# One ring for all PSUM banks and pairs in an eight-core decoder step, and a narrower wait ahead of its down projections

## The chip, the cores and the metric

The kernel runs on the 8 cores of one Trainium2 chip. Each core works on its own tokens with all weights, and no core talks to another. Five engines run side by side on a core: TensorE (PE, matmuls), VectorE (DVE), ScalarE (ACT), GpSimd (POOL, here only the issue of weight loads) and SyncE (SP, the issue of all other transfers). They wait for each other by semaphores only. TensorE writes its results to PSUM, which has 8 banks of 128 partitions x 512 fp32; VectorE or ScalarE must have read a bank before TensorE may write it again. The metric is the device time of one execution in microseconds, that of the slowest core; less is better.

## What is computed

One layer over 2048 prompt tokens and 128 sample tokens a core, width 1024. The reference, cut to what matters:

```python
def swiglu(x, w_gate, w_up, w_down):
    return (jax.nn.silu(x @ w_gate) * (x @ w_up)) @ w_down          # hidden width 2816

def layer(x, p_emb, conv_prev, ...):
    h = x + 0.5 * rmsnorm(swiglu(rmsnorm(x, ffn1_pre_g), ...), ffn1_post_g)
    n = rmsnorm(h, mix_pre_g)
    proj = n @ w_in                                                 # b_a, c_a, h_a, u, v, 512 each
    conv_out, new_conv = causal_dwconv(conv_prev, c_a * h_a, conv_w)
    y_a = b_a * conv_out
    v_n = rmsnorm(v.reshape(B, L, HEADS_B, HEAD_DIM_B), v_norm_g)
    mixed = chunk_spatial_mix(v_n, w_s, b_s)                        # 128 positions a chunk
    y_b = (u * mixed)
    y = jnp.concatenate([rmsnorm(y_a, out_g_a), rmsnorm(y_b, out_g_b)], axis=-1) @ w_out
    h = h + rmsnorm(y, mix_post_g)
    h = h + 0.5 * rmsnorm(swiglu(rmsnorm(h, ffn2_pre_g), ...), ffn2_post_g)
    gate = jax.nn.sigmoid(h @ ple_w_gate)
    h = h + rmsnorm(gate * (p_emb @ ple_w_proj), ple_post_g)
    return h, new_conv, v_cur
```

## The kernel before

The tokens of a core go through the whole layer in two passes: pass 0 has 9 blocks of 128 tokens in 3 tiles of 384, pass 1 has 8 blocks in 2 tiles of 512 (PASSES). A pass has these stages, and each engine does its part of them in the order in which the program is written:

- **Gate and up, feature-major** (gu_stage, gu_unit). Weights are the stationary operand, a tile of normalised tokens nT the moving one. A unit is a gate group and an up group of 8 matmuls, each into one bank from get_bank. ScalarE makes SiLU of the gate bank into one of two buffers sg, VectorE multiplies with the up bank into hmid (in tile "big"). The last product's event is kept in hm["ev"]. Weights lie in a ring of 8 slots; the first two or three are used for all tiles in turn, the others slot by slot.
- **Down, token-major** (tok_stage, proj_block). Per block, two banks make a pair (a tensor ps0 to ps3) from get_pair: 44 matmuls, then ScalarE squares the pair for the norm (post_stat), VectorE scales it into zsc and adds it to h (post_apply), and the next stage's norm makes a bf16 block nbr, which a transposing DMA on SP's queue brings into nT (pre_fn). The block waits for hm["ev"].
- **Mixer**: projections into single banks, a statistic by matmuls with ones (stat, line 707), the spatial mix (line 803), the product with u. The norm of a tile (norm_stat, norm_apply) is made one tile later; that of the last tile follows block 0 of the out projection (tail, with a bank from get_tp).
- **Out projection, token-major** (tok_stage with 16 matmuls a block), then the second gate and up and down stages as above.
- **Embedding stage** (ple), in groups of three blocks: three gate projections into pairs, a sigmoid of each on ScalarE; three embeddings (embed, 4 matmuls each) into pairs, the product on VectorE; then norm, add and y store. In pass 0 it also prepares pass 1: x_square squares the first input tile on ScalarE once its load has landed, x_stat sums it by 8 matmuls (line 498) into a bank from get_tp, which is held until x_apply has read it in the second group. The second tile of pass 1 is prepared inside the first gate and up stage of pass 1.

The hidden units of a stage lie in the same memory as the blocks that ple stores: guard1 makes the first products of pass 1 wait for the y stores of blocks 6, 7 and 8.

What decides who waits for a bank: there are three counters over the same 8 banks. get_bank takes all 8 in turn by rot["all"]; get_pair takes pairs ps0, ps1, ps2 by rot["pair"], always these three but in the last group of pass 1; get_tp takes the two banks of ps3 by rot["tp"]. Each goes on from where it last stood, whatever the others used meanwhile.

Of the kernel before, what the change touches and what calls it, by code (L numbers as in the profile page):

```python
# [14 lines left out]
NFF = 22  # L15
# [86 lines left out]
class Pass:  # L102
# [15 lines left out]
def build_program():  # L118
# [65 lines left out]
    rot = {"all": 0, "pair": 0, "tp": 0}  # L184

    def get_bank():
        b = banks[rot["all"] % 8]
        rot["all"] += 1
        assert b.free is not None
        PE.wait(b.free)  # L190
        b.free = None
        return b

    def get_tp():
        b = banks[6 + rot["tp"] % 2]
        rot["tp"] += 1
        assert b.free is not None
        PE.wait(b.free)
        b.free = None
        return b  # L200
# [222 lines left out]
    hm = {"ev": None}  # L423

    def gu_unit(P, f, fev, j0, ti, guard, hook=None):
# [3 lines left out]
        for jj in range(2):  # L429
# [60 lines left out]
    def x_stat(P, ti, sq, bank_of):  # L490
        c0, w = P.tiles[ti]
        bank = bank_of()
# [7 lines left out]
        e1 = act([ev], out=bank.t[:, 0:w], in_=bank.t[:, 0:w], func=AF.Ln, bias=EPS, scale=0.5)  # L500
        return bank, act([e1], out=bank.t[:, 0:w], in_=bank.t[:, 0:w], func=AF.Exp, scale=-0.5)
# [29 lines left out]
    def proj_block(P, b, nk, lhs, per, fl, wait, release_as_used, npair=3):  # L531
        pair = get_pair(npair)
# [50 lines left out]
    def mixer(P):  # L583
# [119 lines left out]
        def stat(sqs, w, bank_of=get_bank):  # L703
            bank = bank_of()
# [127 lines left out]
        def tail(ev):  # L832
            norm_apply(nt - 1, norm_stat(nt - 1, get_tp))
# [7 lines left out]
    def ple(P, N, base, pT_ev, groups):  # L841
# [8 lines left out]
        def embed(b, last, npair=3):  # L850
            pair = get_pair(npair)
# [12 lines left out]
        for gi, grp in enumerate(groups):  # L864
# [4 lines left out]
            if early:  # L869
                emb = {b: embed(b, b == grp[-1], 4) for b in grp}  # L870
            for b in grp:
                pair, ev = proj_block(P, b, 8, lambda k, b=b: nT_t[:, k, b * 128:(b + 1) * 128], 4, fg, [nT_ev[b]],
                                      lastg and b == grp[-1], 4 if early else 3)
# [5 lines left out]
                if N is not None and b == 1:  # L879
                    xs["sq"] = x_square(N, 0)  # L880
# [7 lines left out]
            if N is not None and gi == 1:  # L888
                x_apply(N, 0, *xs["st"], [gate_ev[3]])
# [3 lines left out]
            if N is not None and gi == 0:  # L893
                xs["st"] = x_stat(N, 0, xs["sq"], get_tp)
# [33 lines left out]
    def start_mid():  # L928
        x_apply(PASSES[0], 2, *x_stat(PASSES[0], 2, nx["sq"], get_bank))
# [14 lines left out]
    def next_mid():  # L944
        e = x_apply(PASSES[1], 1, *x_stat(PASSES[1], 1, nx["sq"], get_bank))
# [4 lines left out]
    for P in PASSES:  # L950
# [32 lines left out]
        tok_stage(P, NFF, 6, lambda b, k: hmid[:, k, b * 128:(b + 1) * 128], lambda b: [hm["ev"]],  # L983
# [31 lines left out]
        tok_stage(P, NFF, 6, lambda b, k: hmid[:, k, b * 128:(b + 1) * 128], lambda b: [hm["ev"]],  # L1015
                  base + G2POST, 4.0, 1, 0, cast, {8: next_x} if N is not None else None)
        gain_load(base + NGAIN + GMPRE, [h_ev[P.nb - 1]])
# [107 lines left out]
```

How the kernel before makes its waits and increments, by code:

```python
    def wait(self, *evs):  # L62
        best = {}
        for ev in _flat(evs, []):
            if ev.key not in best or best[ev.key].val < ev.val:
                best[ev.key] = ev
        for ev in best.values():
            if self.seen.get(ev.key, 0) >= ev.val:
                continue
            self.e.wait_ge(ev.sem, ev.val)
            self.seen[ev.key] = ev.val
            if _COLLECT is not None and ev.idx is not None:
                _COLLECT.add((ev.key, ev.idx))
# [1 line left out]
    def mark(self, ins):  # L75
        self.idx += 1
        if _USED is not None and (self.name, self.idx) not in _USED:
            return Ev(self.sem, self.n, self.name, self.idx)
        self.n += 1
        ins.then_inc(self.sem, 1)
        return Ev(self.sem, self.n, self.name, self.idx)
# [8 lines left out]
    def add(self, ins):  # L90
        self.n += 16
        ins.then_inc(self.sem, 16)
        return Ev(self.sem, self.n, self.name)
```

## Time and profile before

| | us |
|---|---|
| median of 3 runs (lowest, highest) | 1360.84 (1359.67, 1381.91) |
| the profiled execution | 1360.08 |
| its span on the slowest core, core 2 | 1359.0 |
| spans of the eight cores | 1348.5 to 1359.0 |
| TensorE busy | 1300.9 |
| VectorE busy | 523.6 |
| ScalarE busy | 410.3 |
| mean DMA rate | 103 GB/s |

Times in the rows below are microseconds from the start of core 2's span. A row of instructions in order of time has its start, its length, engine, line, operation and operands, how many were merged, and in brackets the idle time of the engine ahead of it and what ended that. A matmul's end is modelled. In pass 0 the first down projection runs from 205 to 291, the out projection from 381 to 416, the second from 591 to 676, the embedding stage to 723; in pass 1 they start at 891, 1043, 1234 and 1310.

### The profile page before, as it was taken

How to read it: one execution, taken by the hardware profiler on the slowest of the kernel's cores; microseconds unless marked ns; L12 is line 12 of the kernel's file. 1: busy time of each engine (PE TensorE's matmuls, PEld its weight loads, DVE VectorE, ACT ScalarE, POOL GpSimd, SP SyncE). 2: the span in 40 equal slices, each digit the busy share in tenths (PEclk: the TensorE clock that was granted, in tenths of full speed). 3: DMA queues.
4: the chain of work that ended last, by engine and by line, in shares of the span. 5: the costliest groups of instructions: out<-in, count | busy, mean ns of one | idle time of the engine just before them, and what ended most of it. 6: DMA issues, size and time to landing. Idle time of an engine off the chain costs nothing.

```text
span 1359.0 us, 18605 instructions; the slowest of 8 cores (1348.5 to 1359.0 us)
## 1 busy us (share of the span) xinstructions
PE 1300.9 (96%) x6770; PEld 650.7 (48%) x6770; DVE 523.6 (39%) x691; ACT 410.3 (30%) x858; POOL 94.3 (7%) x185
## 2 busy tenths in 40 slices
PE   6999999999989999999998999999999799999995
PEld 5566654455535666644433344444444344444442
DVE  3322223357776222213356322124467822212337
ACT  3311112344455111111165211123434611111136
POOL 1100000001001100000001000000010010000000
PEclk8999999999989999999989899999999899999998
DMA  9998322129715963231299983421396297433223
GB/s 214 180 211 181 63 47 47 28 57 164 129 26 103 169 108 63 48 69 26 53 201 232 224 160 67 75 43 31 68 166 116 57 158 143 78 56 62 32 39 124
DMA packets 88185, 139.87 MB, mean 103 GB/s; under 512 B 58272, under 2 KB 58528, under 8 KB 87456
## 3 DMA queue, kind: packets, MB, share of 16 engines
q0 software_dynamic: 25296, 90.25, 40.2%
q1 hardware_dynamic: 62800, 48.43, 13.6%
q8 instruction: 56, 0.92, 0.3%
q14 instruction: 33, 0.27, 0.1%
HBM read 206.03 MB, written 9.51 MB: 159 GB/s over the span
## 4 chain that ended last, share of the span: by engine, by line
PE 84%; DVE 6%; DMA 4%; issue 3%; ACT 2%; DVEq 0%; SPq 0%; ACTq 0%
PE ps L218 55%; PE ps L553 24%; PE ps L542 3%; DVE nT L227 2%; DVE zsc L227 2%; DMA h<-xT 1%; DVE big L231 1%; DMA y<-big 1%; DVE big L227 1%; DMA big<-xT 1%; ACT sg L223 1%; PE ps L498 1%; DVE nbr L227 1%; ACT big L223 1%; ACT L223 0%
## 5 line engine op out<-in xcount | busy, mean ns | idle before, releaser
L218 PE MATMUL ps<-nT,ring 128*128 128x384 bf16 (+1 forms) x4160 | 779.5, 349 | 18.8 <-DVE zsc L227 9.1
L218 PEld LDWEIGHTS ps<-nT,ring 128*128 128x128 bf16 x4160 | 407.9, 98 | 386.3 <-issue 35.4
L231 DVE TENSOR_TENSOR big<-ps,sg 128x384 bf16<-128x384 f32 (+1 forms) x220 | 134.1, 611 | 495.2 <-PE ps L218 476.0
L553 PE MATMUL ps<-ring,big 128*128 128x512 bf16 x1320 | 285.5, 379 | 4.4 <-DVE big L231 4.4
L223 ACT ACTIVATE sg<-ps 128x384 f32<-128x384 f32 (+1 forms) x237 | 126.8, 536 | 508.9 <-PE ps L218 499.9
L553 PEld LDWEIGHTS ps<-ring,big 128*128 128x128 bf16 x1320 | 128.9, 98 | 160.8 <-issue 6.0
L259 POOL DMA_DIRECT2D ring<-w x170 | 89.9, 537 | 1088.4 <-PE ps L218 499.6
L223 ACT ACTIVATE big<-ps 128x1024 bf16<-128x1024 f32 (+4 forms) x88 | 75.3, 870 | 222.6 <-PE ps L553 189.9
L227 DVE SCALAR_TENSOR_TENSOR zsc<-ps,st,gains 128x1024 f32<-128x1024 f32 x51 | 65.4, 1282 | 192.0 <-ACT st L223 191.7
L553 PE MATMUL ps<-ring,nT 128*128 128x512 bf16 x480 | 108.3, 386 | 5.7 <-DVE big L231 5.7
L553 PEld LDWEIGHTS ps<-ring,nT 128*128 128x128 bf16 x480 | 47.4, 99 | 65.6 <-issue 12.0
L231 DVE TENSOR_TENSOR big<-ps,big 128x384 f32<-128x384 f32 (+3 forms) x77 | 50.1, 686 | 46.3 <-PE ps L858 22.7
L231 DVE TENSOR_TENSOR h<-h,zsc 128x1024 f32<-128x1024 f32 x51 | 62.5, 1226 | 5.7 <-DVE zsc L227 0.5
L227 DVE SCALAR_TENSOR_TENSOR nbr<-h,st,gains 128x1024 bf16<-128x1024 f32 x34 | 43.6, 1282 | 36.9 <-ACT st L223 36.9
L223 ACT ACTIVATE nbr<-h 128x1024 bf16<-128x1024 f32 x34 | 35.9, 1057 | 60.3 <-DVE h L231 52.0
L223 ACT ACTIVATE st<-st 128x1 f32<-128x1 f32 x204 | 41.4, 203 | 18.2 <-ACT st L223 0.4
L542 PE MATMUL ps<-ring,big 128*128 128x512 bf16 x176 | 38.6, 379 | 0.0
L223 ACT ACTIVATE big<-big 128x384 bf16<-128x384 f32 (+2 forms) x44 | 25.0, 604 | 39.6 <-DVE big L231 37.1
L223 ACT ACT_TABLE_LOAD x25 | 32.1, 1283 | 13.5 <-PE ps L553 5.9
L218 PE MATMUL ps<-ring,nT 128*128 128x512 bf16 x136 | 30.2, 379 | 0.0
L227 DVE SCALAR_TENSOR_TENSOR nT<-big,gc,zsc 128x384 bf16<-128x384 f32 (+1 forms) x40 | 23.9, 666 | 9.0 <-ACT zsc L223 9.0
L542 PEld LDWEIGHTS ps<-ring,big 128*128 128x128 bf16 x176 | 17.2, 98 | 20.8
(65 smaller groups left out, 365.2 us busy)
## 6 DMA issues: line engine op xcount, KB each, us to landing
ring<-w POOLq DMA_DIRECT2D x170, 512.0 KB, 14.3
h<-x SPq DMA_DIRECT2D x17, 512.0 KB, 28.0
y<-big SPq DMA_DIRECT2D x13, 512.0 KB, 3.4
gains<-gain SPq DMA_DIRECT2D x12, 512.0 KB, 10.0
h<-xT SPq DMA_DIRECT2D x3, 1536.0 KB, 16.6
big<-xT SPq DMA_DIRECT2D x2, 2048.0 KB, 14.7
y<-zsc SPq DMA_DIRECT2D x4, 512.0 KB, 2.9
big<-pT POOLq DMA_DIRECT2D x2, 512.0 KB, 8.0
```

The costliest lines, as they stand in the source:

```text
L218: ins = nc.tensor.matmul(out_ap, l, r, start=(i == 0), stop=(i == n - 1))
L223: return ACT.mark(nc.scalar.activation(**kw))
L227: return DVE.mark(nc.vector.scalar_tensor_tensor(out=out, in0=in0, scalar=scalar, in1=in1, op0=op0, op1=op1))
L231: return DVE.mark(nc.vector.tensor_tensor(out=out, in0=in0, in1=in1, op=op))
L259: nc.gpsimd.dma_start(out=ring_t[:, s, o:o + HALF], in_=w_d[f % NFILL, :, o:o + HALF])))
L498: ins = nc.tensor.matmul(bank.t[:, 0:w], ones_t[:], sqt[:, k, :], start=(k == 0), stop=(k == 7))
L542: ins = nc.tensor.matmul(o.t, lhs(k), sv[:, k % per, half * 512:half * 512 + 512], start=(k == 0), stop=(k == nk - 1))
L553: ins = nc.tensor.matmul(o.t, lhs(k), sv, start=(k == 0), stop=(k == nk - 1))
```

## The change

All PSUM banks and pairs now come from one counter, rot["n"]. get_bank takes the next bank, get_pair the next pair of an even and an odd bank, leaving one out where the counter is odd; so a pair stage goes over all four pairs, and what is handed out is always what was handed out longest ago, but for a bank left out. get_tp is gone. In the embedding stage of pass 0 the statistic of pass 1's first tile no longer holds a bank: x_stat writes its Ln and Exp to the first half of a gain slot (dst), and the gain that belongs there is loaded after x_apply instead of at the end of the down stage. x_square there stands behind the third sigmoid instead of the second, and waits for the last block's h (guards["zsc"]). Last, gu_unit keeps the product's event per tile, and a down block waits for that of its own tile.

```diff
     def __init__(self, idx, rows, tiles, sample):
...
+    def tile_of(self, b):
+        return [ti for ti in range(len(self.tiles)) if b in self.blocks(ti)][0]
...
-    rot = {"all": 0, "pair": 0, "tp": 0}
-
-    def get_bank():
-        b = banks[rot["all"] % 8]
-        rot["all"] += 1
+    rot = {"n": 0}
+
+    def take(b):
         assert b.free is not None
         PE.wait(b.free)
         b.free = None
         return b
 
-    def get_tp():
-        b = banks[6 + rot["tp"] % 2]
-        rot["tp"] += 1
...
-    def get_pair(n=3):
-        i = rot["pair"] % n
-        rot["pair"] += 1
-        lo, hi = banks[2 * i], banks[2 * i + 1]
-        assert lo.free is not None and hi.free is not None
-        PE.wait(lo.free, hi.free)
-        lo.free = hi.free = None
-        return ps[i], lo, hi
+    def get_bank():
+        i = rot["n"] % 8
+        rot["n"] += 1
+        return take(banks[i])
+
+    def get_pair():
+        i = (rot["n"] + 1) // 2 % 4
+        rot["n"] = 2 * i + 2
+        return ps[i], take(banks[2 * i]), take(banks[2 * i + 1])
...
-            hm["ev"] = tt([ev_s, evl, guard(j)], hmid[:, j, cols], bu.t[:, 0:w], sg_t[:, si, 0:w], ALU.mult)
-            bu.free = hm["ev"]
-            sg_free[si] = hm["ev"]
+            e = hm[ti] = tt([ev_s, evl, guard(j)], hmid[:, j, cols], bu.t[:, 0:w], sg_t[:, si, 0:w], ALU.mult)
+            bu.free = sg_free[si] = e
...
-        e1 = act([ev], out=bank.t[:, 0:w], in_=bank.t[:, 0:w], func=AF.Ln, bias=EPS, scale=0.5)
-        return bank, act([e1], out=bank.t[:, 0:w], in_=bank.t[:, 0:w], func=AF.Exp, scale=-0.5)
+        if dst is None:
+            e1 = act([ev], out=bank.t[:, 0:w], in_=bank.t[:, 0:w], func=AF.Ln, bias=EPS, scale=0.5)
+            return bank, act([e1], out=bank.t[:, 0:w], in_=bank.t[:, 0:w], func=AF.Exp, scale=-0.5)
+        bank.free = e1 = act([ev], out=dst, in_=bank.t[:, 0:w], func=AF.Ln, bias=EPS, scale=0.5)
+        return Bank(dst), act([e1], out=dst, in_=dst, func=AF.Exp, scale=-0.5)
...
-                if N is not None and b == 1:
-                    xs["sq"] = x_square(N, 0)
+                if N is not None and b == 2:
+                    xs["sq"] = x_square(N, 0, [guards["zsc"]])
...
             if N is not None and gi == 1:
-                x_apply(N, 0, *xs["st"], [gate_ev[3]])
+                gain_load(base + NGAIN + GMPRE, [x_apply(N, 0, *xs["st"], [gate_ev[3]])])
...
             if N is not None and gi == 0:
-                xs["st"] = x_stat(N, 0, xs["sq"], get_tp)
+                xs["st"] = x_stat(N, 0, xs["sq"], gain(base + NGAIN + GMPRE)[:, 0:512])
...
-        tok_stage(P, NFF, 6, lambda b, k: hmid[:, k, b * 128:(b + 1) * 128], lambda b: [hm["ev"]],
+        tok_stage(P, NFF, 6, lambda b, k: hmid[:, k, b * 128:(b + 1) * 128], lambda b, P=P: [hm[P.tile_of(b)]],
                   base + G2POST, 4.0, 1, 0, cast, {8: next_x} if N is not None else None)
-        gain_load(base + NGAIN + GMPRE, [h_ev[P.nb - 1]])
         guards["zsc"] = h_ev[P.nb - 1]
```

TensorE's order at the out projection of pass 0, before: the last two products with u (into ps3 and ps0), block 0, the last tile's statistic (line 707), and blocks 1 to 3. "Waits" names the semaphores that stand ahead of a matmul: sem_dve is VectorE's, sem_act ScalarE's, slots are weights, t0 and t1 transposes.

```order
L218 MATMUL ps3<-nT,ring 128x384 [waits sem_dve]
L218 MATMUL ps3<-nT,ring 128x384 x7
L218 MATMUL ps0<-nT,ring 128x384 [waits sem_dve]
L218 MATMUL ps0<-nT,ring 128x384 x7
L553 MATMUL ps0<-ring,nT 128x512 [waits sem_dve,slot6_0,slot6_1]
L553 MATMUL ps0<-ring,nT 128x512 x3
L553 MATMUL ps0<-ring,nT 128x512 [waits slot7_0,slot7_1]
L553 MATMUL ps0<-ring,nT 128x512 x11
L707 MATMUL ps3<-big,ones 128x384 [waits sem_act] x4
L553 MATMUL ps1<-ring,nT 128x512 x16
L553 MATMUL ps2<-ring,nT 128x512 x16
L553 MATMUL ps0<-ring,nT 128x512 [waits sem_dve]
```

The same place after the change:

```order
L212 MATMUL ps1<-nT,ring 128x384 [waits sem_dve]
L212 MATMUL ps1<-nT,ring 128x384 x7
L212 MATMUL ps1<-nT,ring 128x384 [waits sem_dve]
L212 MATMUL ps1<-nT,ring 128x384 x7
L549 MATMUL ps2<-ring,nT 128x512 [waits sem_dve,slot6_0,slot6_1]
L549 MATMUL ps2<-ring,nT 128x512 x3
L549 MATMUL ps2<-ring,nT 128x512 [waits slot7_0,slot7_1]
L549 MATMUL ps2<-ring,nT 128x512 x11
L703 MATMUL ps3<-big,ones 128x384 [waits sem_dve,sem_act]
L703 MATMUL ps3<-big,ones 128x384 [waits sem_act] x3
L549 MATMUL ps0<-ring,nT 128x512 [waits sem_dve]
L549 MATMUL ps0<-ring,nT 128x512 x15
```

Block 0 stands in ps2 instead of ps0, which the last product with u has just been using, the statistic in the low bank of ps3, and block 1 in ps0.

TensorE's order from the last block of pass 1's out projection (line 542) into its second gate and up stage, before:

```order
L542 MATMUL ps0<-ring,nT 128x512 [waits sem_dve]
L542 MATMUL ps0<-ring,nT 128x512 x15
L218 MATMUL ps0<-nT,ring 128x512 [waits sem_dve,slot4_0,t1,t0]
L218 MATMUL ps0<-nT,ring 128x512 x7
L218 MATMUL ps1<-nT,ring 128x512 x8
L218 MATMUL ps1<-nT,ring 128x512 [waits slot4_1]
L218 MATMUL ps1<-nT,ring 128x512 x7
L218 MATMUL ps2<-nT,ring 128x512 x8
L218 MATMUL ps2<-nT,ring 128x512 [waits slot5_0]
L218 MATMUL ps2<-nT,ring 128x512 x7
```

And after:

```order
L538 MATMUL ps1<-ring,nT 128x512 [waits sem_dve]
L538 MATMUL ps1<-ring,nT 128x512 x15
L212 MATMUL ps2<-nT,ring 128x512 [waits sem_dve,slot4_0,t1,t0]
L212 MATMUL ps2<-nT,ring 128x512 x15
L212 MATMUL ps3<-nT,ring 128x512 [waits sem_dve,slot4_1]
L212 MATMUL ps3<-nT,ring 128x512 x15
L212 MATMUL ps0<-nT,ring 128x512 [waits sem_dve,slot5_0]
L212 MATMUL ps0<-nT,ring 128x512 x15
L212 MATMUL ps1<-nT,ring 128x512 [waits sem_dve,slot5_1]
L212 MATMUL ps1<-nT,ring 128x512 x15
```

The first gate group was in ps0, the pair of the last block itself; now it is in ps2, and the last block's ps1 comes round as the fourth pair.

ScalarE's order in the first group of pass 0's embedding stage, before (big<-ps are sigmoids, big<-big the squares of x_square, sg,st<-big the norm's squares, ps<-ps the Ln and Exp of x_stat):

```order
L223 ACTIVATE big<-ps 128x1024 x2
L223 ACTIVATE big<-big 128x1024 x4
L223 ACTIVATE big<-ps 128x1024
L223 ACTIVATE sg,st<-big 128x1024
L223 ACTIVATE st<-st 128x1 x2
L223 ACTIVATE sg,st<-big 128x1024
L223 ACTIVATE st<-st 128x1 x2
L223 ACTIVATE sg,st<-big 128x1024
L223 ACTIVATE st<-st 128x1 x2
L223 ACTIVATE ps<-ps 128x512 x2
```

And after:

```order
L217 ACTIVATE big<-ps 128x1024 x3
L217 ACTIVATE big<-big 128x1024 x4
L217 ACTIVATE sg,st<-big 128x1024
L217 ACTIVATE st<-st 128x1 x2
L217 ACTIVATE sg,st<-big 128x1024
L217 ACTIVATE st<-st 128x1 x2
L217 ACTIVATE sg,st<-big 128x1024
L217 ACTIVATE st<-st 128x1 x2
L217 ACTIVATE gains<-ps 128x512
L217 ACTIVATE gains<-gains 128x512
```

The third sigmoid moved ahead of the four squares, and Ln and Exp write gains.

## Rows read from the trace of the kernel before

**Rows 1.** The page, its head and part 1.

```profile
span 1359.0 us, 18605 instructions; the slowest of 8 cores (1348.5 to 1359.0 us)
...
PE 1300.9 (96%) x6770; PEld 650.7 (48%) x6770; DVE 523.6 (39%) x691; ACT 410.3 (30%) x858; POOL 94.3 (7%) x185
```

**Rows 2.** TensorE's waits: total us, times, longest us.

```profile
PE ps L553 <- DVE big L231: 10.0, 6, 4.3
PE ps L218 <- DVE zsc L227: 9.1, 3, 7.0
```

**Rows 3.** TensorE in order of time, pass 0.

```profile
204.96 76.13 PE L553 MATMUL ps<-ring,big 128*128 128x512 bf16 x352 [1.02 <-DVE big L231]
...
381.02 6.48 PE L553 MATMUL ps<-ring,nT 128*128 128x512 bf16 x16 [4.29 <-DVE big L231]
...
387.98 24.34 PE L553 MATMUL ps<-ring,nT 128*128 128x512 bf16 x112
...
421.99 167.86 PE L218 MATMUL ps<-nT,ring 128*128 128x384 bf16 x1032 [0.96 <-DVE zsc L227]
```

**Rows 4.** TensorE in order of time, pass 1.

```profile
891.24 66.64 PE L553 MATMUL ps<-ring,big 128*128 128x512 bf16 x308 [1.16 <-DVE big L231]
...
1042.99 3.61 PE L553 MATMUL ps<-ring,nT 128*128 128x512 bf16 x16 [1.40 <-DVE big L231]
...
1047.30 20.88 PE L553 MATMUL ps<-ring,nT 128*128 128x512 bf16 x96
...
1078.59 154.35 PE L218 MATMUL ps<-nT,ring 128*128 128x512 bf16 x704 [6.95 <-DVE zsc L227]
```

**Rows 5.** TensorE in order of time, from pass 0 to pass 1.

```profile
691.97 1.87 PE L858 MATMUL ps<-ring,big 128*128 128x512 bf16 x4 [3.38 <-ACT big L223]
693.63 3.62 PE L498 MATMUL ps<-big,ones 128*128 128x512 bf16 x8
...
728.80 15.34 PE L218 MATMUL ps<-nT,ring 128*128 128x512 bf16 x64 [5.38 <-DVE big L231]
...
753.58 0.38 PE L218 MATMUL ps<-nT,ring 128*128 128x512 bf16 x1 [0.79 <-DVE nT L227]
```

**Rows 6.** Busy time by stretch: all engines, then TensorE's granted clock, DMA share, GB/s.

```profile
1080.00:1084.00 4.00, 4.00 (x13) 1.42 (x11) 1.93 (x2) 3.30 (x6) 0.13 (x1) 0.60 0.35 68
```

**Rows 7.** VectorE and ScalarE in order of time, 364 to 436, pass 0.

```profile
371.88 2.68 DVE L227 SCALAR_TENSOR_TENSOR big<-ps,gc,bbc 128x256 f32<-128x256 f32 x8
...
378.71 1.94 DVE L231 TENSOR_TENSOR big<-ps,big 128x384 f32<-128x384 f32 x4
...
380.78 1.33 ACT L223 ACTIVATE big<-big 128x384 bf16<-128x384 f32 x3
...
426.95 0.87 ACT L223 ACTIVATE sg<-ps 128x384 f32<-128x384 f32 x2
```

**Rows 8.** ScalarE, SP and VectorE in order of time, 664 to 762.

```profile
687.03 3.90 ACT L223 ACTIVATE big<-big 128x1024 bf16<-128x1024 f32 x4 [2.49 <-DMA big<-xT]
...
732.18 5.38 SPq L901 DMA_DIRECT2D y<-big  x3
...
752.08 0.69 DVE L231 TENSOR_TENSOR big<-ps,sg 128x512 bf16<-128x512 f32 x1 [2.57 <-DMA y<-big]
```

**Rows 9.** DMA issues, 737.1 to 737.6 (block 8's store): count, KB, us to landing.

```profile
y<-big SPq DMA_DIRECT2D x1, 512.0 KB, 14.8
```

**Rows 10.** DMA queues, 744 to 746: packets, MB, share; q0 weights, q1 SP.

```profile
q0 software_dynamic: 75, 0.25, 74.6%
q1 hardware_dynamic: 71, 0.28, 36.1%
```

**Rows 11.** ScalarE in order of time, 1030 to 1090.

```profile
1072.73 1.06 ACT L223 ACTIVATE nbr<-h 128x1024 bf16<-128x1024 f32 x1 [0.38 <-DMA nT<-nbr]
```

**Rows 12.** Transposes of that stretch: us from issue to landing.

```profile
DMA to landing us min/median/max: 3.0/3.0/9.8
```

**Rows 13.** Chain of work that ended last: start, us, what.

```profile
1346.69 1.23 DVE big L231
```

More of the change, by code:

```diff
@@ L192, in get_bank @@
         return b
-    def get_tp():
-        b = banks[6 + rot["tp"] % 2]
-        rot["tp"] += 1
[L197 to L200, printed above, removed]
-    def get_pair(n=3):
-        i = rot["pair"] % n
-        rot["pair"] += 1
-        lo, hi = banks[2 * i], banks[2 * i + 1]
-        assert lo.free is not None and hi.free is not None
-        PE.wait(lo.free, hi.free)
-        lo.free = hi.free = None
-        return ps[i], lo, hi
+    def get_bank():
[6 more added lines that the diff above has]
+        return ps[i], take(banks[2 * i]), take(banks[2 * i + 1])
     def mm_group(out_ap, pairs, wait=None, kwait=None):
@@ L422, in build_program @@
     sgc = {"i": 0}
-    hm = {"ev": None}
+    hm = {}
     def gu_unit(P, f, fev, j0, ti, guard, hook=None):
@@ L488, in x_square, with x_stat @@
         return sq
-    def x_stat(P, ti, sq, bank_of):
+    def x_stat(P, ti, sq, dst=None):
         c0, w = P.tiles[ti]
-        bank = bank_of()
+        bank = get_bank()
         sqt = x_sq_at(P, ti)
@@ L529, in post_apply, with proj_block @@
         return e
-    def proj_block(P, b, nk, lhs, per, fl, wait, release_as_used, npair=3):
-        pair = get_pair(npair)
+    def proj_block(P, b, nk, lhs, per, fl, wait, release_as_used):
+        pair = get_pair()
         pt, lo, hi = pair
@@ L701, in square, with stat @@
             return i, e
-        def stat(sqs, w, bank_of=get_bank):
-            bank = bank_of()
+        def stat(sqs, w):
+            bank = get_bank()
             for c, (i, e) in enumerate(sqs):
@@ L832, in tail @@
         def tail(ev):
-            norm_apply(nt - 1, norm_stat(nt - 1, get_tp))
+            norm_apply(nt - 1, norm_stat(nt - 1))
         return norm_ev, tail, vo_ev["ev"]
@@ L849, in ple, with embed @@
             pay_owed([nT_ev[P.nb - 1]], NFILL + 1)
-        def embed(b, last, npair=3):
-            pair = get_pair(npair)
+        def embed(b, last):
+            pair = get_pair()
             pt, lo, hi = pair
@@ L869, in ple @@
             if early:
-                emb = {b: embed(b, b == grp[-1], 4) for b in grp}
+                emb = {b: embed(b, b == grp[-1]) for b in grp}
             for b in grp:
                 pair, ev = proj_block(P, b, 8, lambda k, b=b: nT_t[:, k, b * 128:(b + 1) * 128], 4, fg, [nT_ev[b]],
-                                      lastg and b == grp[-1], 4 if early else 3)
+                                      lastg and b == grp[-1])
                 gate_ev[b] = ev
@@ L914, in gb_guard @@
         return [guards["zsc"] if b % 6 >= 4 else None, out_ev.get(b - 6) if b >= 6 else None]
-    first = x_stat(PASSES[0], 0, x_square(PASSES[0], 0), get_bank)
+    first = x_stat(PASSES[0], 0, x_square(PASSES[0], 0))
     x_apply(PASSES[0], 0, *first)
-    second = x_stat(PASSES[0], 1, x_square(PASSES[0], 1), get_bank)
+    second = x_stat(PASSES[0], 1, x_square(PASSES[0], 1))
     warm_up(40)
@@ L928, in start_mid @@
     def start_mid():
[L929 removed]
+        x_apply(PASSES[0], 2, *x_stat(PASSES[0], 2, nx["sq"]))
     def start_loads():
```

8 lines of the change are left out of this document (4 added, 4 removed).

## Prediction

> **What bounds the kernel now.** I read the page first, then TensorE's waits, then its instructions in order of time, and last the engines it waits for. The page says that TensorE is busy for 1300.9 of 1359.0 us [rows 1]. So nothing but TensorE's pauses, and matmuls that run slower than others of their shape, can be won without taking matmuls away; the change takes none away. Its longest waits name VectorE, once through tile big and once through zsc [rows 2]: TensorE waits until VectorE has read a bank, or until VectorE has written the last FFN product. In order of time these pauses stand in four kinds of place. (a) At each of the four starts of a down projection: 1.02 us in pass 0 and 1.16 in pass 1 [rows 3, 4], one row of each pass shown. (b) Around the out projection of pass 0: 4.29 us ahead of its first block, and among others 0.96 in the gate and up matmuls behind it [rows 3]. (c) From the embedding stage of pass 0 into pass 1: 3.38, 5.38 and 0.79 us [rows 5]. (d) Around the out projection of pass 1: 1.40 and 6.95 us [rows 4]. Behind the long pauses the clock is at 1.2 GHz for a while: the 16 matmuls of block 0 take 6.48 us in pass 0 and 3.61 in pass 1 [rows 3, 4], and 1080 to 1084 has a granted clock of 0.60 [rows 6]. The pauses of 1.0 to 1.4 us are followed by matmuls at full pace.
>
> **Part 1: the product wait, (a).** A down block now waits for the products of its own tile. Tile 0's last product is four units of work older than the stage's last in pass 0 and two in pass 1, so it is long done, and the pair is the oldest of the ring, used four units ago. The pauses go: 1.02 twice and 1.16 twice. A row's modelled end lies some 0.16 us past the next start (1042.99 + 3.61 is 1046.60, yet four matmuls of 20.88 / 96 us each stand between it and 1047.30 [rows 4]), so a pause costs 0.16 more than it shows. 4 x 0.16 + 4.36 = **5.0**. Nothing stands between these points and the end but TensorE, so all of it arrives.
>
> **Part 2: out projection of pass 0, (b).** Block 0 waited for pair ps0, one bank of which the last product with u still read. In the ring it takes ps2, last read by the mix operations that end at 371.88 + 2.68 = 374.56 [rows 7], while TensorE is free at 381.02 - 4.29 = 376.73. It starts there, at full clock, and ends at 380.0. But behind it stands the statistic of the last tile, whose four matmuls need ScalarE's squares, and these end at 380.78 + 1.33 = 382.11, because VectorE's products end only at 378.71 + 1.94 = 380.65 [rows 7]. So a new pause of 2 us stands there, and block 1 starts at 382.4 instead of 387.98: 5.6 earlier. VectorE's and ScalarE's work of the stage hangs on that statistic and moves by the same 5.6. The gate and up matmuls now start 128 matmuls of 24.17 / 112 us behind block 1's start, at 387.98 + 27.6 - 5.6 = 410.0, and find each pair free, but after 8 groups of 8 matmuls (167.86 us over 1032, so 1.30 a group) the ring is round at 420.4, and bank 0 is free only when ScalarE has made the first SiLU: 426.95 + 0.45 - 5.6 = 421.8 [rows 7]. The stage thus runs as if begun at 411.5. Before, the fourth group began at 421.99, as if begun at 418.1. Gain **6.6**.
>
> **Part 3: embedding stage into pass 1, (c).** The third embedding waited 3.38 us since its pair was freed by a sigmoid that stood behind the four squares of pass 1's input, and these wait for a load until 687.03 [rows 8]. The sigmoid now goes first, so the embedding starts at 688.6; the squares end one sigmoid later, 687.03 + 3.90 + 1.0 = 691.9, and the statistic's last matmul follows at 692.4. The next gates start at 692.6 instead of 693.63 + 3.62 = 697.2 [rows 5]; I take 4.3. Everything up to pass 1 moves with it, and the 5.38 us bank wait ahead of pass 1 goes too, so TensorE reaches pass 1 about 10 us earlier. This is not kept. The second tile of pass 1 waits for its normalised input, which VectorE writes only after the product of 752.08, and that one waits for the y store of block 8 (the unit's output lies where that store reads) [rows 8]. At 753.58 TensorE is already waiting for VectorE [rows 5]. The three stores were issued from 732.18 on, and the last landed 14.8 us after its issue [rows 8, 9]. So the second tile starts when the stores land, and these move with their issue, by 4.3. TensorE's other 6 us become a pause between its eighth bank and the first product. Gain **4.3**.
> The ring order puts a 0.5 MB gain load between the input load and the first of those stores. In 2 us of that time SP's queue moved 0.28 MB and the weight queue 0.25 [rows 10], so 0.5 MB may cost 3.6 us if nothing else gives. I take nothing, since three stores need only 10.8 us at that pace and have 14.8 behind the last issue alone, so the queue has gaps to give; 3.6 stays for the range.
> The Trainium skill (DMA: Bandwidth & Descriptors, Queues, rings and completion order) says that an engine takes turns between queue rows by packet and takes one ring's descriptors in order. The 71 and 75 packets agree [rows 10]. By that rule alone the moved load delays all six later stores, the gain of this part would be 0.7 instead of 4.3, and the whole 1339.3; that is rival A.
>
> **Part 4: out projection of pass 1, (d).** Block 0 no longer waits; the statistic needs squares that end some 0.4 us after block 0. Block 1 starts at 1045.9 instead of 1047.30: 1.4, and VectorE's chain moves as much. The gate and up matmuls waited 6.95 us for the pair of block 7. In the ring that pair is the last they need. What they need first is the transposed block 3, on which ScalarE's instruction at 1072.73 waited [rows 11], so it lands at 1072.6; 1.4 less is 1071.2. So the start goes from 1078.59 to 1071.3, and the pause ahead of it shrinks to 1.2, below those that left the clock alone. Before, about 4.6 us (1078.59 to 1083.2, by the granted clock [rows 6]) ran at half pace: 2.3 lost. Together 7.3 + 2.3 = 9.6. The second tile is wanted 12 groups of 1.73 us later, at 1092.0; block 7's transpose takes 9.8 us where the others take 3.0 [rows 12], since it runs beside the pT load, and lands at 1092.3. That takes back 0.4. Gain **9.2**.
>
> **What gains nothing.** In the last groups of pass 1 the ring removes a short wait, but VectorE is at the b5 block's add until 1346.69 and takes the next embedding with no pause of its own [rows 13]: the tail is VectorE's and ScalarE's, not TensorE's. The statistic's Ln and Exp write SBUF instead of a bank; no row of theirs is on TensorE's way.
>
> **Sum.** 5.0 + 6.6 + 4.3 + 9.2 = 25.1 off a span of 1359.0, so 1333.9. That execution took 1360.08, and the median of the runs is 1360.84, 0.8 more. 1360.84 - 25.1 = **1335.7**, 1.8% faster. A measurement of this kernel can tell about 2% from no change, which is 1333.6 or less.
>
> **The rivals.**
> A, the stores don't move (chance 0.17). For it: the moved gain load, and DMA engines that are full while weights come. Against it: the gaps. The second tile starts at 753 as now: 25.1 - 4.3 = 20.8 gained, 1340.0.
> B, the clock falls in the new pauses (0.15). The statistics of parts 2 and 3 now trickle over 2.4 and 3 us behind squares. Price of a fall: 6.48 - 3.61 = 2.9 us each [rows 3, 4]. For it: pauses of 3.38 and more did it. Against it: those up to 1.4 did not. Both: 25.1 - 5.8 = 19.3, 1341.5; one: 1338.6.
> C, the ring gives nothing (0.04): VectorE and ScalarE set the pace of the out projections, so TensorE only reaches full banks 8 groups later. Against it: in part 2 this costs 1.4 us, worked out above. Only part 1 stays: 1355.8. The Trainium skill (TensorE: Matmul & The Clock Gate, HAM oscillation) reports of one kernel that double buffering in PSUM gave no further gain. Here the trace disagrees, since 6.95 us are spent on one pair.
> D, the stores land earlier still (0.12): without gaps the three take 10.8 us from their first issue at 728, and with some us to get going the last is down by 744, not 747.7. Then the second tile gains 8.5, not 4.3: 29.3, 1331.5.
> E, slower than before (0.02): with fewer pauses the eight cores draw more at once and the clock granted to long stretches falls. At 1300.9 us busy it decides from 1.9% on (25.1 us), and at 4% it would cost 52 and give 1388. No long stretch shows it now.
> F, the forecast (0.50), with its own range of 1332.5 to 1339.
>
> **How the numbers follow.** F's upper part, A and B lie up to 1341.5; the range goes to 1344 for A with one fall of the clock (1342.9), and down to 1331 for D. It leaves out C, E and some of D and of the sums beyond. Below 1333.6 lie D and about a third of F: 0.28. Over 2% slower is E, 0.02. The rest, 0.70, is within 2%.
>
> **What would show it.** Right: the four down starts without a pause; block 0 of pass 0's out projection at 3.5 us and about 2 us of pause behind it; the gate and up stage behind it with one pause of 1 to 2 us at its ninth group; no pause at the third embedding; a pause of 4 to 6 us in pass 1's first tile that ends with a y store; pass 1's second FFN starting on the transpose. Wrong: matmuls of double length behind the statistics (B), the first product of pass 1 more than 12 us behind its store's issue (A), or a bank wait in the middle of a stage.

## The result, and the profile after

| | before | after |
|---|---|---|
| median of 4 runs, us | 1360.26 | 1335.69 |
| lowest run, us | 1357.31 | 1334.43 |
| ratio of the times, 95% interval | | 0.983 (0.9813 to 0.9847) |
| span on the slowest core | 1359.0 (core 2) | 1335.0 (core 7) |
| spans of the eight cores | 1348.5 to 1359.0 | 1329.7 to 1335.0 |

By the ratio the change makes the kernel 1.7% or 23.1 us faster (20.8 to 25.4 by its interval); the medians differ by 24.6, and 25.1 were forecast. The number hides one term that failed: most of what TensorE won on its way into pass 1 was lost again to three stores, and something else made up for it. Some runs of each kernel were disturbed on a die and have longer times; the ratio leaves them out, so it is what I compare below, one experiment in which every run was so has none, and where a profile has such a die only the other cores are read. The page and the waits of TensorE, as in [rows 1, 2]:

```profile
span 1335.0 us, 18647 instructions; the slowest of 8 cores (1329.7 to 1335.0 us)
...
PE 1293.0 (97%) x6770; PEld 649.3 (49%) x6770; DVE 523.4 (39%) x691; ACT 410.5 (31%) x858; POOL 94.3 (7%) x185
```

```profile
PE ps L212 <- DVE big L225: 6.0, 2, 5.8
PE ps L212 <- DVE nT L221: 4.9, 11, 2.1
...
PE ps L212 <- ACT sg L217: 1.5, 1, 1.5
...
PE ps L212 <- DMA nT<-nbr: 1.2, 1, 1.2
```

The two long entries of [rows 2] are gone: nothing of line 549 (553 before) waits for VectorE any more, and no matmul waits for zsc. The 5.8 us are one new pause in pass 1's first tile; only the waits for the first inputs, at the start of the program, are longer in total (8.5 us, 8.9 before).

TensorE in order of time in pass 0, core 7; these rows answer to [rows 3]:

```profile
202.59 76.14 PE L549 MATMUL ps<-ring,big 128*128 128x512 bf16 x352
...
374.19 3.62 PE L549 MATMUL ps<-ring,nT 128*128 128x512 bf16 x16
377.65 0.32 PE L703 MATMUL ps<-big,ones 128*128 128x384 bf16 x1
379.06 1.15 PE L703 MATMUL ps<-big,ones 128*128 128x384 bf16 x3 [1.08 <-ACT big L217]
380.04 24.34 PE L549 MATMUL ps<-ring,nT 128*128 128x512 bf16 x112
...
407.67 10.56 PE L212 MATMUL ps<-nT,ring 128*128 128x384 bf16 x64
419.73 161.36 PE L212 MATMUL ps<-nT,ring 128*128 128x384 bf16 x992 [1.50 <-ACT sg L217]
```

The down projection starts without a pause. Block 0 of the out projection takes 3.62 us instead of 6.48, and the one pause of the gate and up stage comes after 64 matmuls, that is at the ninth group, and waits for the first SiLU. Pass 1, which answers to [rows 4], has lost its bank waits too; its second FFN starts on a transpose:

```profile
877.77 66.64 PE L549 MATMUL ps<-ring,big 128*128 128x512 bf16 x308
...
1028.33 3.61 PE L549 MATMUL ps<-ring,nT 128*128 128x512 bf16 x16 [0.20 <-issue]
...
1032.64 20.88 PE L549 MATMUL ps<-ring,nT 128*128 128x512 bf16 x96
...
1058.15 152.11 PE L212 MATMUL ps<-nT,ring 128*128 128x512 bf16 x704 [1.17 <-DMA nT<-nbr]
```

Between the passes ([rows 5]) the embeddings no longer wait, but the first tile of pass 1 now has a pause of 5.77 us, and the second tile starts with one of 2.05:

```profile
692.75 2.75 PE L854 MATMUL ps<-ring,big 128*128 128x512 bf16 x12
...
708.29 13.98 PE L212 MATMUL ps<-nT,ring 128*128 128x512 bf16 x64
...
730.50 8.60 PE L212 MATMUL ps<-nT,ring 128*128 128x512 bf16 x32 [5.77 <-DVE big L225]
741.14 0.38 PE L212 MATMUL ps<-nT,ring 128*128 128x512 bf16 x1 [2.05 <-DVE nT L221]
```

The same stretch on SP and VectorE. The three stores are issued from 717.35 on, 2.5 us apart, and three products wait for one each; the last is let go at 739.65 by a store issued at about 722.4 ([rows 8] has the one row of before):

```profile
717.35 5.38 SPq L897 DMA_DIRECT2D y<-big  x3
...
729.55 0.69 DVE L225 TENSOR_TENSOR big<-ps,sg 128x512 bf16<-128x512 f32 x1 [7.23 <-DMA y<-big]
...
734.38 1.29 DVE L225 TENSOR_TENSOR big<-ps,sg 128x512 bf16<-128x512 f32 x2 [4.13 <-DMA y<-big]
...
739.65 0.69 DVE L225 TENSOR_TENSOR big<-ps,sg 128x512 bf16<-128x512 f32 x1 [3.99 <-DMA y<-big]
```

Its issue, 722.3 to 722.6, with count, KB and us to landing, as in [rows 9]:

```profile
y<-big SPq DMA_DIRECT2D x1, 512.0 KB, 17.2
```

And the queues while the first two are waiting, 717 to 723 (packets, MB, share of 16 engines), as in [rows 10]; the third is issued in the last of these us:

```profile
q0 software_dynamic: 187, 0.66, 107.5%
q1 hardware_dynamic: 4, 0.00, 0.1%
```

For almost 6 us the stores move nothing: the weight queue has the engines. It moves only 0.66 MB in that time; why its own packets take so long no run shows. What it carries was issued from 710.65 on:

```profile
710.65 3.18 POOL L253 DMA_DIRECT2D ring<-w  x6 [31.19 <-PE ps L212]
```

Then the held-back weight loads, six of 0.5 MB, were let go, since pass 1's second input tile had landed: its load was issued at 693.06 and took 16.9 us. (The row names a matmul as what ended the wait; on four other cores it names that load.) Granted clock (third column from the end) on core 7 in that stretch; the columns are those of [rows 6]:

```profile
720.00:724.00 4.00, 3.73 (x17) 1.35 (x15) 2.22 (x2) 3.99 (x5) 0.00 (x0) 1.00 0.90 81
...
728.00:732.00 4.00, 1.50 (x4) 0.58 (x5) 0.69 (x1) 0.60 (x1) 0.00 (x0) 0.50 0.99 211
732.00:736.00 4.00, 4.00 (x16) 1.54 (x15) 1.29 (x2) 0.82 (x2) 1.05 (x2) 0.83 1.07 212
...
744.00:748.00 4.00, 3.78 (x9) 1.15 (x9) 2.81 (x5) 0.60 (x1) 0.00 (x0) 0.50 0.97 151
748.00:752.00 4.00, 4.00 (x15) 1.51 (x13) 0.69 (x1) 0.00 (x0) 0.00 (x0) 0.69 1.02 199
```

Behind both pauses TensorE is at 1.2 instead of 2.4 GHz for some us.

### The profile page after: what moved, and what is told of

Same layout as the page of the kernel before. It is cut to its first block, busy times and chain, and to the rows that moved or that the text cites. A ratio compares the mean times of both kernels' runs of the same rounds, so it can differ in the third digit from the quotient of the medians.

```text
span 1335.0 us, 18647 instructions; the slowest of 8 cores (1329.7 to 1335.0 us)
## 1 busy us (share of the span) xinstructions
PE 1293.0 (97%) x6770; PEld 649.3 (49%) x6770; DVE 523.4 (39%) x691; ACT 410.5 (31%) x858; POOL 94.3 (7%) x185
## 4 chain that ended last, share of the span: by engine, by line
PE 87%; DVE 5%; DMA 3%; issue 2%; ACT 2%; DVEq 0%; SPq 0%; ACTq 0%
PE ps L212 56%; PE ps L549 25%; PE ps L538 3%; DMA h<-xT 1%; DVE zsc L221 1%; DMA y<-big 1%; DVE nT L221 1%; PE ps L854 1%; DVE big L221 1%; DVE big L225 1%; DVE nbr L221 1%; PE ps L703 1%; ACT L217 0%; DMA nT<-nbr 0%; ACT big L217 0%
## 5 line engine op out<-in xcount | busy, mean ns | idle before, releaser
L549 PE MATMUL ps<-ring,nT 128*128 128x512 bf16 x480 | 105.2, 379 | 0.2 <-issue 0.2
L212 PE MATMUL ps<-ring,nT 128*128 128x512 bf16 x136 | 30.2, 379 | 0.0
L538 PEld LDWEIGHTS ps<-ring,big 128*128 128x128 bf16 x176 | 17.2, 98 | 20.8
L221 DVE SCALAR_TENSOR_TENSOR big<-big,gc 128x384 f32<-128x384 f32 (+3 forms) x48 | 24.8, 589 | 0.0
## 6 DMA issues: line engine op xcount, KB each, us to landing
big<-xT SPq DMA_DIRECT2D x2, 2048.0 KB, 12.4
```

What stands on the lines that cost most here:

```text
L212: ins = nc.tensor.matmul(out_ap, l, r, start=(i == 0), stop=(i == n - 1))
L221: return DVE.mark(nc.vector.scalar_tensor_tensor(out=out, in0=in0, scalar=scalar, in1=in1, op0=op0, op1=op1))
L538: ins = nc.tensor.matmul(o.t, lhs(k), sv[:, k % per, half * 512:half * 512 + 512], start=(k == 0), stop=(k == nk - 1))
L549: ins = nc.tensor.matmul(o.t, lhs(k), sv, start=(k == 0), stop=(k == nk - 1))
```

## The experiments

All were timed beside the kernel before, whose median was 1357.9 for the first four and 1358.2 for the last four. A difference between two of them is that of their ratios, 0.001 being 1.36 us; each ratio is good to some 2 us, so what is smaller rests on the stretches below. To see where in the program a difference lies I also read, on each core, the time from the start of one down projection to that of the next, in the profiled execution. A is the stretch from pass 0's first to its second, with the mixer and out projection of pass 0; B runs from there to pass 1's first, over the embedding stage and the first FFN of pass 1; C is as A for pass 1. Mean of the cores in us, and for B lowest and highest:

| kernel | ratio (95% interval) | A | B | C |
|---|---|---|---|---|
| before | 1 | 386.1 | 295.9 (293.2 to 300.4) | 342.5 |
| changed | 0.983 (0.9813 to 0.9847) | 378.4 | 294.4 (291.8 to 296.8) | 332.4 |
| product wait alone | 0.9964 (0.995 to 0.9978) | 383.6 | 294.0 (289.6 to 296.6) | 341.7 |
| squares early | 0.9839 (0.9825 to 0.9854) | 378.4 | 293.1 (291.1 to 294.9) | 332.4 |
| gain load late | 0.9829 (0.9815 to 0.9844) | 378.4 | 293.5 (291.9 to 294.3) | 332.3 |
| weight loads late | 0.9745 (0.973 to 0.9759) | 378.4 | 281.9 (281.7 to 282.2) | 332.4 |
| three pairs | 0.9849 (0.9831 to 0.9868) | 378.9 | 294.2 (293.6 to 294.6) | 334.9 |
| weight and gain loads late | 0.9745 (0.9729 to 0.9761) | 378.4 | 281.9 (281.7 to 282.1) | 332.4 |
| before, weight loads late | 0.9971 (0.9959 to 0.9984) | 386.2 | 291.8 (289.8 to 294.1) | 342.9 |
| youngest pair first (six cores) | none | 378.4 | 294.1 (292.1 to 294.7) | 339.8 |

In the changed kernel A and C are the same on all cores within 0.2 us; B is not. It is the stretch in which transfers decide, and it is the same on all cores, within 0.5 us, only in the two kernels that have both the ring and the late weight loads.

**The product wait alone.** The kernel before, with

```diff
-            hm["ev"] = tt([ev_s, evl, guard(j)], hmid[:, j, cols], bu.t[:, 0:w], sg_t[:, si, 0:w], ALU.mult)
+            hm["ev"] = hm[ti] = tt([ev_s, evl, guard(j)], hmid[:, j, cols], bu.t[:, 0:w], sg_t[:, si, 0:w], ALU.mult)
...
-        tok_stage(P, NFF, 6, lambda b, k: hmid[:, k, b * 128:(b + 1) * 128], lambda b: [hm["ev"]],
+        tok_stage(P, NFF, 6, lambda b, k: hmid[:, k, b * 128:(b + 1) * 128], lambda b, P=P: [hm[P.tile_of(b)]],
```

> The kernel before with part 1 alone: a down block waits for the last product of its own tile; the three counters for the banks stay. Theory of the prediction: the four down starts lose their pause, 5.0 us in all, and nothing else moves, so the time goes from 1360.3 to 1355.3 (ratio 0.9963). Rival: the two starts of pass 0 (2.4 us) lie ahead of the way into pass 1, where TensorE waits for transfers, and are given back there; then only the two starts of pass 1 count, 2.6 us, 1357.7 (ratio 0.998). A second rival: the three pairs are still handed out by their own counter, and one of the starts now waits for a bank instead, 1.0 to 1.2 us less gain for each such start.

Measured: 0.9964, which is 4.9 us less, and no pause ahead of the down projections. That is what the first theory says; 2.6 would be a ratio of 0.998, just outside the interval. The stretches are less even than the sum. By the four pauses A should be 1.2 shorter, B and C 1.3 each; they are 2.5, 1.9 and 0.8 shorter. In A the other 1.3 us are mostly something else: in the kernel before, five cores reach the out projection 177.7 us behind the start of the down projection and three 176.1, here all eight after 176.0 to 176.2. Why is not shown. So the pauses are gone, but that exactly their price arrives is not proven by this run.

**Squares early.** The changed kernel with

```diff
-                if N is not None and b == 2:
+                if N is not None and b == 1:
```

> The changed kernel with the squares of pass 1's first input behind the second sigmoid again, as in the kernel before (part 3's reordering undone, the rest kept). The prediction put 3.4 of part 3's 4.3 us down to the third sigmoid standing ahead of the squares: then the third embedding waits some 3 us again and the time is 1338 to 1339. Rival: with four pairs in one ring the third embedding takes the pair of the second gate, which the second sigmoid has freed, so the order on ScalarE no longer matters, and the time stays at 1335.7 within 1 us.

Measured: 0.9839 against 0.983, 1.2 us and inside both intervals, and no core has a pause ahead of an embedding. The rival holds. The prediction named the right pause and the wrong cure: it is gone because the ring has four pairs, so that the third embedding writes the pair whose sigmoid is the second, not the third. The order on ScalarE is worth nothing that shows in the time. In the changed kernel the next gates start 5.6 us behind the embeddings on every core (682.40 - 676.76 on core 7). With the old order it is 4.4 to 6.3 and 5.4 on the mean: less where the input had landed early (4.9 on core 3, 681.25 - 676.35), more where the statistic waits for it.

**Gain load late.** The load that the change had moved is issued behind the y stores:

```diff
-                gain_load(base + NGAIN + GMPRE, [x_apply(N, 0, *xs["st"], [gate_ev[3]])])
+                xs["ap"] = x_apply(N, 0, *xs["st"], [gate_ev[3]])
...
         gain_load(base + GPLE + 3, [nxt["stt"]])
+        if N is not None:
+            gain_load(base + NGAIN + GMPRE, [xs["ap"]])
```

> The changed kernel with the moved 0.5 MB gain load issued behind the y stores of pass 0 instead of ahead of the second group's. If it delays the stores that pass 1 waits for (rival A of the prediction), taking it away gives up to 3.6 us back: 1332.1. Theory after reading the changed kernel's trace: SP's queue has run empty before the last three stores are issued (nothing of it moves between 717 and 723 on core 7), so the load delays at most the input load beside it; 1335.0, 0 to 1.5 us better.

Measured: 0.9829 against 0.983; B is 0.9 shorter on the mean of the cores, less than the cores differ. Whether it is 0 or 1 us stays open. The 3.6 us of the prediction's bound (a ratio of 0.9804) lie outside the interval.

**Weight loads late.** The changed kernel, with the six weight loads that are let go ahead of pass 1's FFN let go by another event:

```diff
-            pay_owed([xt_ev[1, 1]])
+            pay_owed([out_ev[8]])
```

pay_owed lets the held-back loads go, in GpSimd's queue, once its event has come: before, the landing of pass 1's second input tile, here that of block 8's y store.

> The changed kernel with the six weight loads of 0.5 MB that were held back until the second input tile of pass 1 had landed now held back until the y store of block 8 has landed. Theory: what keeps pass 1's first tile waiting (5.8 + 2.1 us of pauses on core 7 and 4 to 6 us at half clock behind them) are the last three stores, 12 to 17 us each, and they are slow because the weight queue takes 70 to 120% of the DMA engines' time in that stretch. Without it a store lands in 4 to 6 us, TensorE goes through the first tile without a pause of over 1 us, and gate and up of pass 1 take 155 to 159 us instead of 167 to 169.5: 1323 to 1328 (ratio to the kernel before 0.973 to 0.976). Rival 1: the stores are slow for another reason: no change, 1335.7. Rival 2: the fourth weight slot comes too late, and TensorE waits for weights at about 750 instead: 1333 to 1340.

Measured: 0.9745, 34.6 us less than before and 11.5 less than the changed kernel, as the theory says. B falls by 12.5 on the mean, and its spread between cores from 5.0 to 0.5 us. TensorE on the slowest core, core 1:

```profile
709.83 13.98 PE L212 MATMUL ps<-nT,ring 128*128 128x512 bf16 x64
723.64 1.69 PE L491 MATMUL ps<-nT,ones 128*128 128x512 bf16 x6
725.68 0.59 PE L491 MATMUL ps<-nT,ones 128*128 128x512 bf16 x2 [0.35 <-ACT nT L217]
726.11 8.58 PE L212 MATMUL ps<-nT,ring 128*128 128x512 bf16 x39
```

The 5.77 us pause is gone. First the row of the weight loads, which block 8's store now lets go; then the three stores, issued from 718.88 to 723.9, with count, KB and us to landing, and the clock behind them:

```profile
727.41 3.17 POOL L253 DMA_DIRECT2D ring<-w  x6 [45.43 <-DMA y<-big]
```

```profile
y<-big SPq DMA_DIRECT2D x3, 512.0 KB, 2.8
```

```profile
724.00:728.00 4.00, 3.58 (x17) 1.32 (x15) 2.54 (x4) 3.84 (x5) 0.59 (x2) 1.00 0.79 241
728.00:732.00 4.00, 4.00 (x20) 1.81 (x19) 2.57 (x4) 3.51 (x6) 2.58 (x5) 1.00 0.66 116
```

A store now lands 2.8 us after its issue (median of the three, the others 2.6 and 3.9), not 12 to 17, and the clock stays at 2.4 GHz. Both rivals are out: the stores were slow for the weight loads' sake, and the weights, issued at 727.4, come in time, since no matmul of core 1 waits for them.

**Three pairs.** The changed kernel with one counter, but projections over three pairs:

```diff
-    def get_pair():
-        i = (rot["n"] + 1) // 2 % 4
+    def get_pair(n=4):
+        i = (rot["n"] + 1) // 2 % 4 % n
...
-        pair = get_pair()
+        pair = get_pair(npair)
```

where proj_block has npair=4 as its default and tok_stage passes 3. So the down and out projections go over three pairs; the gate projections of the embedding stage call proj_block without it and keep four, although the text written ahead of the run says three.

> The changed kernel, its one counter kept, but the blocks of every down, out and gate projection go over three pairs only (where the ring stands at ps3, it goes on to ps0); embeddings and single banks still use all. It tells the fourth pair from the order. Theory: within a stage VectorE is at most two blocks behind TensorE, so a third-oldest pair is free when it is wanted, and what counts is that a stage begins on the oldest bank and not on the youngest: time of the changed kernel, 1335.7 within 1 us. Rival: the fourth pair itself gives the gain of the out projections, and without it a bank wait comes back inside them or ahead of gate and up: 3 to 8 us slower, 1339 to 1344.

Measured: 0.9849 against 0.983, 2.6 us slower. The two intervals overlap; the stretches, A 0.5 longer and C 2.5, say the same more sharply. It is neither the theory's 1 us nor the rival's 3 to 8. On core 5:

```profile
PE ps L549 <- DVE zsc L221: 3.7, 2, 2.1
```

One pause of 1.59 us in pass 0 and one of 2.15 in pass 1, each ahead of the third block of an out projection and none behind it. The statistic behind block 0 takes a bank of the second pair, so with three pairs block 1 gets the third and block 2 is back at block 0's, only two blocks old. My theory missed the statistic. And the pause of 2.15 costs more than itself:

```profile
1037.77 19.11 PE L549 MATMUL ps<-ring,nT 128*128 128x512 bf16 x80 [2.15 <-DVE zsc L221]
```

```profile
1036.00:1040.00 4.00, 2.23 (x7) 0.87 (x8) 3.90 (x4) 2.14 (x5) 0.00 (x0) 0.82 0.02 4
1040.00:1044.00 4.00, 4.00 (x16) 1.65 (x15) 2.57 (x3) 1.49 (x5) 0.00 (x0) 0.76 0.00 1
```

At full pace 80 of these matmuls take 17.4 us (20.88 for 96 in the changed kernel), so 1.7 are lost to the clock. 2.15 + 1.7, less the 1.2 us wait for the transpose that is then gone, is 2.6, and C is 2.5 longer. On core 6 the clock did not fall behind the same pause, and C is only 1.0 longer there. The fourth pair is worth this, but for 0.5 us in A all of it at this one block; the rest of what the ring gives is order.

**Youngest pair first.** The changed kernel with

```diff
+        if P.idx == 1:
+            rot["n"] = 2
         gu_stage(P, 3, guard_none)
```

> The changed kernel with the ring set back by one pair ahead of the second gate and up stage of pass 1, so that its first group stands in the pair of the last out-projection block (ps1), as in the kernel before, and nothing else changed. Theory of part 4: TensorE then waits until VectorE has read that pair, at 1062.2 + 1.3 = 1063.5 instead of starting at 1058.15 on core 7, 5.3 us, a pause of 6.5, and behind a pause of that length some 4 to 5 us of matmuls run at half pace, 2.3 more: 7.6 slower, 1343.3. Rival 1: the low clock had another cause than the pause: only 5.3, 1341.0. Rival 2: the transposes and not the bank set the start (they were there before as well): no change.

There is no ratio; the table has the mean of cores 0, 1 and 4 to 7 in the profiled execution (C from 339.4 to 340.9). C is 7.4 longer than in the changed kernel, against 7.6 by the theory and 5.3 or 0 by the rivals; 5.8 of it are the longer pause (6.95 against 1.17), 1.7 the slower matmuls behind it (153.77 us for 704 against 152.11). On core 5:

```profile
1062.03 153.77 PE L212 MATMUL ps<-nT,ring 128*128 128x512 bf16 x704 [6.95 <-DVE zsc L221]
```

```profile
1060.00:1064.00 4.00, 1.97 (x5) 0.74 (x6) 3.90 (x4) 1.50 (x4) 0.00 (x0) 0.50 0.38 68
1064.00:1068.00 4.00, 4.00 (x16) 1.65 (x15) 1.46 (x3) 3.43 (x6) 0.23 (x1) 0.82 0.61 70
```

The pause is back at 6.95, to the hundredth that of [rows 4], and so is the low clock. That settles part 4: the wait was for the bank and not for the transposes, and the clock behind it is part of its price. The Trainium skill (TensorE: Matmul & The Clock Gate, HAM oscillation) tells of a kernel in which double buffering in PSUM gave nothing further; here the order of the same eight banks is worth 7.4 us at one place.

**Weight and gain loads late.** Both edits together.

> The changed kernel with both the held-back weight loads behind block 8's y store (e4_fills_late) and the 0.5 MB gain load behind the y stores (e3_gain_late). In e4_fills_late the first tile of pass 1 had no pause left over 0.3 us at its banks and the stores landed 4.4 to 5 us after their issue, so the gain load is in nobody's way any more. Theory: 1323.3, as e4_fills_late, within 0.7 us. Rival: the gain load costs what it did in e3_gain_late, 1.0 us: 1322.3.

Measured: 0.9745, B 281.9: the theory holds, the gain load is in nobody's way. (The stores' 4.4 to 5 us in that text were misread; they land after 2.6 to 3.9.)

**Before, weight loads late.** The kernel before with the one line of the weight loads changed.

> The kernel before with the same delay of the six weight loads as in e4_fills_late and nothing of the change. It tells what the delay is worth without the ring. Theory: in the kernel before TensorE reaches pass 1 ten us later and waits 5.4 us for a bank there, so the slow stores cost it only the 0.8 us pause ahead of the second tile, the small ones behind it and the low clock at 748 to 764; the delay gives 3 to 6 us, 1352 to 1355, and the ring and the delay together (34.6 us in e4_fills_late) give 6 to 9 us more than their single gains (22.2 and this one) add up to, which are the us that part 3 of the change won on TensorE and lost to the stores. Rival: the two gains are independent: the delay gives 12.4 us here as well, 1345.5.

Measured: 0.9971, 3.9 us less, B shorter by 4.1. The theory holds. Ring and delay, each alone, give 23.1 + 3.9 = 27.0, together 34.6: 7.6 us come only when both are there. In B, with the 1.3 of the down start taken off both, the ring wins 291.8 - 1.3 - 281.9 = 8.6 us where the stores are out of the way, and 295.9 - 1.3 - 294.4 = 0.2 where they are not.

## Why the prediction was right, and where it was not

The ledger between the two profiled executions, core 2 before and core 7 after, each gain read from the start of the same work:

| | forecast | measured |
|---|---|---|
| part 1, down starts | 5.0 | 5.0 |
| part 2, out projection of pass 0 | 6.6 | 6.4 |
| part 3, into pass 1 | 4.3 | 2.2 |
| part 4, out projection of pass 1 | 9.2 | 9.2 |
| start of the program, not forecast | | 1.2 |
| sum, and the spans' difference | 25.1 | 24.0 |

**Part 1 was right.** The down starts have no pause, and alone they give 4.9 by the ratio, if unevenly by stretches.

**Part 2 was right in each step.** Block 0 starts 4.5 us earlier at full pace (4.3 forecast), block 1 5.6 earlier (5.6), and the ninth group waits 1.50 for ScalarE (1.4). The pause at the statistic shows 1.08, not 2: one of its four matmuls runs ahead of it, and block 1 starts where it was put. The gap to 6.6 is at the ninth group, which starts at 419.73, 0.3 later than its 421.8 less the 2.4 us gained earlier; behind it nothing is lost up to the second down projection.

**Part 3 was wrong in two steps and half right in size.** Its first half, on TensorE, came as forecast, though not by the sigmoid's move: the next gates start 4.7 earlier (4.3 forecast, 4.6 by its own rows), pass 1 10.6 earlier (about 10), and the first tile has the pause that ends with a y store. The step that failed is "these move with their issue". From the old trace to the new one the last store's issue moved from 737.2 to 722.4, by 14.8, and its landing only from 752.0 to 739.6, by 12.4, since it took 17.2 us instead of 14.8. "The queue has gaps to give" was read from two us, 744 to 746 [rows 10], and was false of the stretch in which the stores were to lie: there the weight queue took 107% and SP's queue 0.1%. Rival A saw that danger: it named both the moved gain load and engines that are full of weights, but took its price of 3.6 us from the gain load, which costs 0 to 1 us. What counts are the six weight loads, which a landed input lets go just ahead of the stores: 9.2 us ahead of the first store in the old trace (722.97 and 732.18), 6.7 in the new one. The sign that the prediction named for A, a first product more than 12 us behind its store's issue, came on core 7, by a hair (12.2 us; 9.5 to 11.5 on the others), and yet the stores did move, by half of what they should. Rival D, stores without gaps, was the opposite of what happened; it needed the weight loads to stop, as in the fourth experiment. (Its sum also has a slip: a last store at 744 instead of 747.7 adds 3.7 to the 4.3, which is 8.0 and not 8.5.)

The Trainium skill (DMA: Bandwidth & Descriptors, Queues, rings and completion order) says that an engine takes turns between queue rows by packet. From 723 to 740 the trace agrees, with 499 and 458 packets. From 717 to 723 it shows no taking of turns, 187 and 4 with two stores issued; whether the engines had packets of these stores to choose from by then, it does not show.

The second step was to take core 2's trace for all. It was the slowest in large part because it lost most just here: its third embedding waited 3.38 us [rows 5], where core 5's waited 2.0, and behind it core 2 had a granted clock of 0.83, 0.50 and 0.82 in the 4 us windows from 688 to 700, core 5 one of 1.00. On the mean of the cores part 3 kept 0.2 us. The metric takes the slowest core, and so it also gained what the spread lost: the spans went from 10.5 us apart to 5.3, and their mean fell by 20.1 us where the slowest fell by 24.0.

**Part 4 was right**, and the sixth experiment shows it by itself. Block 1 starts 1.2 earlier (1.4), gate and up 7.0 (7.3), and 2.2 us of low clock are avoided (2.3). The 0.4 us for block 7's transpose did not come, there is no pause ahead of the second tile.

**Nothing came from the tail**, as forecast: TensorE's last matmuls start 25.5 us earlier (1342.62, 1317.15) and the span ends 24.0 earlier, so the last 1.5 were VectorE's and ScalarE's.

**Rival B** was half there, in another place. No clock fell at the statistics (1.00 in every 4 us from 372 to 388, from 676 to 688 and from 1024 to 1036, where the pauses are 1.1 us and less). It fell in the new 5.8 us pause, which the prediction had itself put there and not priced. Its price of a fall, 2.9 us, was again core 2's: on core 4 of the same kernel the 16 matmuls took 4.97 us behind the same pause, not 6.48, which makes it 1.4. C was out, since 7.4 us hang on one pair (youngest pair first), and so was E: the mean granted clock of the eight cores is 0.987 to 0.990, and it was 0.980 to 0.987.

**What the sum owes to luck.** 1.2 us of the ledger came from the start of the program, where TensorE's first weights and inputs land and the change does nothing. Without them 22.8 stand against the 25.1 of the forecast. It is a matter of which cores are compared: on the mean of the eight, the first down projection starts 0.6 us later after the change once its pause is taken off. And part 3, read from the one core on which it was largest, was made up for in the metric by the narrower spread. So the mechanism of parts 1, 2 and 4 was right, and that 1335.69 us were measured where 1335.7 had been forecast is luck.

## What to carry to other kernels

Hand out buffers by age, over all stages together: a stage that begins on its predecessor's youngest buffer waits for that buffer's reader, and here it paid again in the clock (5.8 and 1.7 us). Where a gain ends at a transfer, ask what is let go just ahead of that transfer; one event moved by some us was worth 11.5 us here, half as much as the whole change, and it was worth 3.9 as long as TensorE arrived late. Read a stretch that depends on transfers on all cores before a number is taken from it.

## What the hardware showed

- A 0.5 MB store on SP's queue landed 2.6 to 3.9 us after its issue when both queues were empty (fourth experiment, core 1, issued from 718.88 on), 6.3 to 8.8 when the weight queue was empty but SP's own queue still had an input load of 2 MB under way (the three stores before those, issued from 706.87 on), and 12.1 to 17.2 when six weight loads of 0.5 MB had been issued from 6.7 us ahead of the first one on (changed kernel, core 7). Of the longer time of the first store, the first 6 us passed with 4 packets moved.
- The length of a pause of TensorE alone does not tell whether slow matmuls follow it. All pauses of 1.5 to 1.6 us at the ninth group and ahead of pass 0's third block (three-pair experiment) were followed by full pace. One of 2.15 us in the three-pair experiment was followed by slow matmuls on seven cores of eight (19.11 us for 80) and by none on core 6 (17.43 for 79). Those of 3.0 us and more in pass 1's first tile of the changed kernel were followed by a 4 us window of granted clock 0.50 to 0.73 on every core. But ahead of the third embedding a pause of 2.87 us (kernel before, core 0) and one of 3.52 (first experiment, core 7) were followed by a clock of 1.00 for 8 us, and one of 3.38 (kernel before, core 2) by one of 0.50.
- What a fall costs is not fixed either: in the kernel before, the 16 matmuls behind the pause of 4.3 us in pass 0 took 6.48 us on core 2, 6.57 on core 3, 5.3 on cores 1, 5 and 7 and 4.97 on core 4, where 3.6 is full pace.
